# Rope halves swapped by ScalarE copies in the dilated layer, with shorter stick-breaking sums and a later weighing of attention pairs

## What is computed

```python
def rope_2(x, pos, rot_dim):        # heads of 64: half = 32
    ...
    x1, x2 = xr[..., :half], xr[..., half:]
    rot = jnp.concatenate([x1 * cos - x2 * sin, x2 * cos + x1 * sin], axis=-1)
    ...

def stick_breaking_attention(q, k, v):          # first block, 4 heads
    ...
        log_not = jnp.where(mask, -jax.nn.softplus(z), 0.0)
        after = lax.cumsum(log_not, axis=3, reverse=True) - log_not
        w = jnp.where(mask, jnp.exp(jax.nn.log_sigmoid(z) + after), 0.0)
        outs.append(jnp.einsum("bhqk,bkhd->bqhd", w.astype(v.dtype), v[:, :end]))
```

## Time and profile before

| | us |
|---|---|
| three runs | 3425.69, 3422.81, 3422.94 (median 3422.94) |
| profiled execution | 3417.32 |
| span of its trace | 3416.0 |
| PE busy in it | 3322.6 (97%) |
| DVE / ACT / POOL busy | 1709.5 / 717.5 / 2415.8 |
| share of PE in the chain that ended last | 88% |
| granted TensorE clock, mean | 0.994 |

### The profile page before, as it was taken

One profiled execution on the slowest core, in us unless ns is written; L12 is line 12 of the kernel. 1 busy time (PEld: TensorE's weight loads), 2 busy tenths in 40 slices (PEclk: granted clock), 3 DMA queues, 4 the chain that ended last, 5 costly groups with the idle time before them and its releaser, 6 DMA issues.

```text
span 3416.0 us, 42138 instructions
## 1 busy us (share of the span) xinstructions
PE 3322.6 (97%) x15386; PEld 2628.0 (77%) x15389; DVE 1709.5 (50%) x1889; ACT 717.5 (21%) x1447; POOL 2415.8 (71%) x1115
## 2 busy tenths in 40 slices
PE   8999999999999999999999999998999999999998
PEld 7888775788887888776678887674788877778887
DVE  5454444554657546154464574688554234454521
ACT  3111125311114111123421113316211101331100
POOL 8888762588886888865278887660688786548875
PEclk9999999999999999999999999999999999999999
DMA  3223220222332223322022233220222222112232
GB/s 132 98 94 106 92 87 32 87 86 98 108 129 71 91 98 102 117 70 79 32 87 98 98 110 109 93 87 1 80 93 98 99 103 100 65 56 96 95 104 93
DMA packets 84367, 305.15 MB, mean 89 GB/s; under 512 B 9360, under 2 KB 9616, under 8 KB 83984
## 3 DMA queue, kind: packets, MB, share of 16 engines
q1 hardware_dynamic: 80928, 292.59, 25.3%
q10 hardware_dynamic: 3312, 10.86, 0.9%
HBM read 299.22 MB, written 4.19 MB: 89 GB/s over the span
## 4 chain that ended last, share of the span: by engine, by line
PE 88%; DVE 6%; ACT 3%; issue 3%; DMA 0%; DVEq 0%; ACTq 0%
PE psC L600 12%; PE psC L602 12%; PE psC L601 12%; PE psA L600 8%; PE psA L602 8%; PE psA L601 8%; PE psB L600 5%; PE psB L601 5%; PE psB L602 5%; PE psC L1072 1%; PE psC L1073 1%; PE psC L1074 1%; DVE stat L1811 1%; DVE X L1600 1%; DVE HL L1584 1%
## 5 line engine op out<-in xcount | busy, mean ns | idle before, releaser
L524 POOL TENSOR_TENSOR WH<-raw,scalars 128x1024 fp32r<-128x1024 f32 (+1 forms) x554 | 1049.5, 1894 | 931.9 <-DMA raw<-in_w 864.0
L526 POOL TENSOR_TENSOR WL<-raw,WH 128x1024 fp32r<-128x1024 f32 (+1 forms) x554 | 1363.7, 2462 | 43.4
L600 PE MATMUL psA<-HH,WH 128*128 128x512 f32 x1136 | 454.3, 400 | 2.2 <-DVE PROJ L1903 2.2
L602 PE MATMUL psA<-HL,WH 128*128 128x512 f32 x1136 | 442.9, 390 | 0.0
L601 PE MATMUL psA<-HH,WL 128*128 128x512 f32 x1136 | 442.7, 390 | 0.0
L600 PE MATMUL psC<-HIDH,WH 128*128 128x512 f32 x1056 | 416.1, 394 | 0.0
L602 PE MATMUL psC<-HIDL,WH 128*128 128x512 f32 x1056 | 414.0, 392 | 0.0
L601 PE MATMUL psC<-HIDH,WL 128*128 128x512 f32 x1056 | 409.8, 388 | 0.0
L1673 DVE TENSOR_TENSOR HIDL<-Y,HIDH 128x512 f32 (+1 forms) x132 | 258.9, 1961 | 125.7 <-ACT HIDH L1314 125.7
L600 PE MATMUL psC<-HH,WH 128*128 128x512 f32 x704 | 275.9, 392 | 0.0
L601 PE MATMUL psC<-HH,WL 128*128 128x512 f32 x704 | 274.3, 390 | 0.0
(11 more groups left out here) (370 smaller groups left out, 4798.9 us busy)
## 6 DMA issues: line engine op xcount, KB each, us to landing
raw<-in_w SPq DMA_DIRECT2D x554, 512.0 KB, 3.3
X<-in_x ACTq DMA_DIRECT2D x4, 512.0 KB, 9.0
NRAW<-in_mem ACTq DMA_DIRECT2D x2, 1024.0 KB, 5.3
out<-Y SPq DMA_DIRECT2D x8, 256.0 KB, 2.1
POSI<-in_pos ACTq DMA_DIRECT2D x4, 256.0 KB, 2.7
PRAW<-in_p ACTq DMA_DIRECT2D x2, 512.0 KB, 3.6
table_F<-newF ACTq DMA_DIRECT2D x2, 512.0 KB, 3.4
table_I<-newI ACTq DMA_DIRECT2D x2, 512.0 KB, 4.4
```

The lines of the kernel that those rows point to most:

```text
L524: pool.tensor_tensor(WH[j][:, 0:w], raw[j][:, 0:w], zero[:, 0:1].broadcast_to([P, w]), ALU.subtract).then_inc(w_hi, 1)
L526: pool.tensor_tensor(WL[j][:, 0:w], raw[j][:, 0:w], WH[j][:, 0:w], ALU.subtract).then_inc(w_split, 1)
L600: pe.matmul(out, WH[slot][:, w], hi[:, t], start=start and t == 0, stop=False)
L602: mm = pe.matmul(out, WH[slot][:, w], lo[:, t], start=False, stop=stop and t == tiles - 1)
```

## The change

Three edits. First, in the dilated layer PE no longer makes the rotated copies. ACT makes them by `swap_halves`: four copies of 32 partitions by 512 for each rope, the lower half from the upper with scale -1 and the upper from the lower, from SBUF into the same two banks. ACT waits until DVE has taken the rope's piece (`pj_done`) and until the bank is free (`rot_done`, that is, until the rope two before has been turned). DVE's `turn` waits for `swap_ready` in place of `rot_ready`.

Second, `r` of stick-breaking sums over two blocks at most, b and b+1. Before that DVE adds, for b=1 and b=0, block b+2 onto block b+1 for both heads at once (`add_later_block`), and PE waits for it (`later_ready`) ahead of the first head.

Third, `ahead_of` gives a third distance, and in "dsa" and "mem_dil" PE weighs pair j-5 instead of pair j-4; ACT's and DVE's copies at the ends of groups move with it, and the loops run one iteration longer.

```diff
+    def dil_ropes_at(p):
+        first = p // 6 * 4 + 2 * (p % 6 - 4)
+        return (first, first + 1)
...
     def ahead_of(which):
 
-        return 2, 3
+        return 2, 3, 1 if which == "mla" else 2
...
             def r(i):
                 c, b, x = SB_UNITS[i]
                 pe.wait_ge(zsp_ready, n.full(zsp_ready))
-                for k in range(b, QB):
+                if x == 0 and b < QB - 2:
+                    pe.wait_ge(later_ready, n.full(later_ready))
+                for k in range(b, min(b + 2, QB)):
...
-            for j in range(len(pairs) + late + 1):
+            for j in range(len(pairs) + late + weighed_late):
...
-                if j - late - 1 >= 0:
-                    weigh(j - late - 1)
+                if j - late - weighed_late >= 0:
+                    weigh(j - late - weighed_late)
...
             for p in range(2, IN_DIL):
                 next_piece(p)
-                g, c = p // 6, p % 6
-                if g < 3 and c >= 4:
-                    rotate(ropes[4 * g + 2 * (c - 4):4 * g + 2 * (c - 4) + 2])
                 if 4 <= p < 8:
                     memory_squares(p - 4)
...
+        def swap_halves(ropes, p):
+
+            for r in dil_ropes_at(p):
+                act.wait_ge(pj_done, chunks_before + 6 * (r // 4) + r % 4 + 1)
+                act.wait_ge(rot_done, n.room(rot_done))
+                for h in range(0, P, HD):
+                    low, high = slice(h, h + HD // 2), slice(h + HD // 2, h + HD)
+                    act.activation(PC[low, r % 2], ropes[r][0][high], ACT.Copy, scale=-1.0)
+                    swapped = act.activation(PC[high, r % 2], ropes[r][0][low], ACT.Copy)
+                swapped.then_inc(swap_ready, 1)
...
-            squares([NRAW[:, k] for k in range(KD)], MS_Y, D, YSS, w=MEM)
+            if kind == "dsa":
+                squares([NRAW[:, k] for k in range(KD)], MS_Y, D, YSS, w=MEM)
+            else:
+                n.full(rot_done, EARLIER_ROPES)
+                ropes = rope_list("dil")
+                for p in (4, 5):
+                    swap_halves(ropes, p)
+                squares([NRAW[:, k] for k in range(KD)], MS_Y, D, YSS, w=MEM)
...
                 for k in range(KD):
                     memory_high(k)
+                for p in (10, 11, 16, 17):
+                    swap_halves(ropes, p)
...
+            def add_later_block(u):
+
+                b = SB_PAIRS[u][1]
+                if b >= QB - 2:
+                    return
+                own = slice(sb_at(b + 1) + P, sb_at(b + 1) + sb_w(b + 1))
+                later = slice(sb_at(b + 2), sb_at(b + 2) + sb_w(b + 2))
+                dve.wait_ge(e_ready, e_base + 2 * u)
+                dve.tensor_tensor(SBL[:, :, own], SBL[:, :, own], SBL[:, :, later], ALU.add).then_inc(later_ready, 1)
+
             e_base = n.now(e_ready)
-            for u in range(len(SB_PAIRS)):
+            for u in range(len(SB_PAIRS) + 1):
+                if u > 0:
+                    add_later_block(u - 1)
+                if u == len(SB_PAIRS):
+                    break
```

More of the change, by code:

```diff
@@ L842, in r @@
                 pe.wait_ge(zsp_ready, n.full(zsp_ready))
[L843 removed]
+                if x == 0 and b < QB - 2:
+                    pe.wait_ge(later_ready, n.full(later_ready))
+                for k in range(b, min(b + 2, QB)):
                     o = sb_bank(i)[:, (k - b) * P:]
                     at = slice(sb_at(k), sb_at(k) + sb_w(k))
[L846 removed]
+                    mm = pe.matmul(o, tri if k == b else onen, SBL[:, x, at], start=False, stop=k == min(b + 1, QB - 1),
+                                   skip_group_check=True)
                 mm.then_inc(e_ready, 1)
@@ L988, in attend @@
             pairs = pairs_of(which)
-            ahead, late = ahead_of(which)
+            ahead, late, weighed_late = ahead_of(which)
             pe.wait_ge(rot_done, n.now(rot_done))
@@ L1476, in attend @@
                     copy_turned(j - late)
-                group = ended_group(which, j - late)
+                finished = j - late - weighed_late + 1
+                group = ended_group(which, finished)
                 if group is not None:
-                    act.wait_ge(pv_done, used_base + j - late)
+                    act.wait_ge(pv_done, used_base + finished)
                     out, bank = heads_out(OH, PD[:, group % 2], which, group)
@@ L1524, in _ @@
             pieces = IN_DSA if kind == "dsa" else IN_DIL
+            chunks_before = n.now(pj_done)
             n.full(piece_used, pieces + 4)
@@ L1785, in convolution_step, with turn @@
             n.full(dve_step)
-        def turn(ropes, bank=None, first=0):
+        def turn(ropes, bank=None, first=0, swapped=False):
             for v, (src, rows, tab, perm) in enumerate(ropes):
-                dve.wait_ge(rot_ready, n.full(rot_ready))
+                if swapped:
+                    dve.wait_ge(swap_ready, n.full(swap_ready))
+                else:
+                    dve.wait_ge(rot_ready, n.full(rot_ready))
                 got = (PC[:, (first + v) % 2] if bank is None else bank)[0:rows]
@@ L1832, in attend @@
                     last_sums(j)
-                group = ended_group(which, j - late)
+                group = ended_group(which, j - late - weighed_late + 1)
                 if group is not None:
```

10 lines of the change are left out of this document (6 added, 4 removed).

## The result

The changed kernel takes 3440.32 us (median of 6 runs, 3433.45 to 3444.98) beside 3422.88 for the kernel before: a ratio of 1.0046, interval 1.0035 to 1.0058. The forecast was 3425.5, the range ended at 3431.5. The profiled execution took 3433.84 us, its span is 3432.5, 16.5 more than before.

What follows compares the result with a forecast made beforehand. PE, busy 97% of the span, was taken as the bound. Edits of +0.3, +4.8 and -2.5 summed to +2.6 on the median 3422.94, giving 3425.5 us, with a range of 3416 to 3431.5.

Steps and rivals of the forecast that it cites:

- Rotations off PE: Dilated layer's projection: six pairs of rotations leave PE at 1.77 us each, -10.6 us.
- The wait at piece 4: Dilated layer's projection: PE waits for memory squares queued behind ACT's copies of ropes 0 to 3, +9.3 us (6.2 to 10.4).
- The clock behind it: Dilated layer's projection: a slow-clock stretch after PE's stall at piece 4, +1.6 us, bounds 0 and twice that.
- Edit one as a whole: Dilated layer's projection: rotations removed, PE's stall and slow clock together, +0.3 us, between -4.4 and +3.0.
- The addition: Stick-breaking, block 0: DVE's addition over 2x256 elements takes 0.68 us alone and 1.57 beside POOL.
- The sums of the last block: Stick-breaking, block 0: PE's shortened sums take 3.0 us instead of 4.53, a saving of 1.5.
- Edit two together: Stick-breaking: -1.0 + 1.8 + 1.6 = +2.4 us a layer, +4.8 for two layers, between -1.1 and +5.7.
- The later weighing: Dsa layer and memory heads: fewer PE waits for transposed weights, -1.0 and -1.5, together -2.5 us, between -10.7 and 0.
- (a): Rival: low clock lasts longer, a second slow stretch after each of three stalls, +4.8 to 3430.3 us; chance .13.
- (b): Rival: the later weighing in dsa layer and memory heads gives all of its 10.7 us, 3417.3; chance .10.
- (c): Rival: PE's wait at piece 4 doesn't arise, the first edit gives its full 10.6 us, 3414.6; chance .07.

Runs made afterwards that it cites:

- ropes_fixed: First edit alone, with ACT's memory squares made between the rope copies, against the kernel before: 3412.29 us beside 3422.68, ratio 0.9968.
- sums_alone: Second edit alone (shorter sums with DVE's addition), against the kernel before: 3432.81 us beside 3423.17, ratio 1.0029.
- sums_weigh: Second and third edits without the first, against the kernel before: 3433.64 us beside 3425.10, ratio 1.0026.
- squares_between: Whole change with ACT's memory squares made between the rope copies; timed against the kernel before: 3423.59 us beside 3423.17, ratio 0.9999.

## Why the prediction was wrong

- **Rotations off PE, -10.6: right.** -10.4 when nothing covers it (ropes_fixed).
- **The wait at piece 4, +9.3: right**, 9.66, by the links named. A copy of 32 partitions took 0.59, as the row of 128 partitions that was taken (0.58). The four took 2868.27 - 2865.87 = 2.40 us together. The prediction's estimate for them by the Trainium skill, "ScalarE: Activation LUTs", section "What ACT_TABLE_LOAD costs", was 2.2; the row gave 2.3, and the trace lies nearer to the row.
- **The clock behind it, +1.6: too small**, 3.1 of the bound's 3.2. Edit one as a whole was forecast at +0.3 and measured -1.0, with its interval from -4.1 to +2.0.
- **The addition, 0.68 to 1.57 us: the step that failed.** The upper end came from one row, DVE's product beside POOL, and was treated as a bound. It is none: that product too stood until 0.55 behind the end of POOL's instruction, of which 1.02 was left when it began. In the last block POOL had just begun an instruction of 2.34, and the addition lasted 2.69. POOL's instructions in the trace of before would have given the bound: 1.90 and 2.35 for the next, so up to 2.9 with the 0.55. With 2.69 the wait of PE is 5.0 and not 2.4 to 3.3; about 0.45 of these 5.0 is what PE saves at block 1 just before, and is no loss.
- **The sums of the last block, 3.0 us: right at full clock only**, 3.25 there. In chunk 1, behind the wait, they took 4.7 to 6.1 in all seven traces with DVE's addition ahead of block 0; the forecast had 4.6, with its 1.6 of clock. In chunk 0 they ran at full clock except in the first layer of both traces of the whole change (4.94), where a gain of 1.0 became a loss of 1.2; the waits ahead of them are as short in the other traces.
- **Edit two together** was forecast at +2.4 a layer and lost 4.1 by the trace of sums_alone: 4.6 to 4.9 in chunk 1 in place of 3.4, of which the addition is 1.1, and a gain of 0.6 in chunk 0 in place of 1.0. By the medians it is +9.6 against +4.8.
- **The later weighing, -2.5 between -10.7 and 0: wrong in sign for dsa**, +2.7 by the traces against -1.0. That the waits would come back elsewhere was right. That an iteration more at the end costs nothing was not: the bound of 0 rested on its having no new instruction, but the end has no scores left to put between, so PE waits 2.47 there and then runs slow. The memory heads gained 1.7, as said (1.5).
- **The rivals.** (a), the low clock lasting longer, came about in part: the clock was low for longer than one stretch behind the wait at piece 4 and in the second layer's last sums (5.78 us), but not in the first layer's. It was priced at 4.8 and does not reach the result. (b) and (c) did not happen.
- **The sum.** +2.6 was forecast, the edits one by one give +9.3, and the whole gives +14 to +17. So the known failings (4.8 in the sums, about 3 in the weighing, less 1.3 in the ropes) explain 6.7 of the 14.8 between forecast and result; the rest is the open part above. The profiled execution doesn't show all of it: at 3433.84 it is 11.0 above the median of before, and the median of the six runs lies 6.5 above it.

## What to carry to other kernels

An instruction that moves to an idle engine is priced by what stands behind it in that engine's list and by who waits for that: here eight small squares behind sixteen copies cost PE all that the copies had saved, and the same copies with the squares between them gave the whole gain. A short DVE operation on two SBUF operands that PE waits for is priced by the longest POOL instruction that can be under way and 0.55 us, as measured here, not by a row in which it happened to meet a short remainder. Before a pipeline is made one step deeper, look at its end, where the fill is missing.

## What the runs showed of the hardware that was not expected

- DVE's addition of two SBUF operands ended 0.55 us behind the end of POOL's running instruction wherever it stood (1.38, 1.99 and 2.69 us for the same 512 elements; 28 additions in seven traces). With 256 elements it ended 0.28 behind, and took 0.41 where POOL was idle at its start.
- The granted clock was at half during a wait of 9.66 us and for 6.4 us behind it, and near half behind two waits of under 1 us in stick-breaking (0.57). The latter came in both traces of the whole change, but not in sums_alone, sums_weigh and squares_between, whose waits there are as long (0.92 to 0.93, then 0.48 to 0.57): the same sums take 3.25 us in them. In the kernel before a wait of 2.23 us was followed by one slow stretch.
- An ACT copy from SBUF to PSUM of 32 partitions by 512 took 0.59 us, as long as one of 128 partitions (0.58).
